# Another order of wide and narrow matmuls inside the units of the seven long sections of a two-layer encoder trunk

## The reference, cut to what matters

```
x = x + attention_layer(rms_norm(x, ...), ...)        # layer 0: its last step is  concat([o_a, o_b]) @ w_out      -> "out0"
x = x + rglru_layer(rms_norm(x, ...), ...)            # layer 1: proj = h @ w_in -> "rec"; (gelu(gate)*y) @ w_out  -> "out1"
x = x + memory_cross_attention(...)                   # both layers
def conv_ffn(h, w_up, conv_w, conv_b, w_down):        # both layers
    u = causal_depthwise_conv(h @ w_up, conv_w, conv_b)          # "up0", "up1"
    val, gate = jnp.split(u, 2, axis=-1)
    return (jax.nn.gelu(gate) * val) @ w_down                    # "down0", "down1"
```

## Time and profile before

| what | value |
|---|---|
| median of 3 runs | 2329.73 us (2328.11 to 2332.1) |
| the profiled execution's own time | 2328.69 us |
| its span | 2327.0 us |
| TensorE (PE) matmul busy | 2299.9 us, 99% |
| VectorE (DVE) busy | 1582.4 us, 68% |
| ScalarE (ACT) busy | 1237.3 us, 53% |
| mean share of the 16 DMA engines | about 55% |
| granted TensorE clock | 0.999 of full, so 2.4 GHz |

### The profile page before, as it was taken

How to read it: one execution, slowest core, us unless ns; L and a number is a source line. 1 busy time by engine, 2 the same in 40 slices (tenths; PEclk the granted TensorE clock), 3 DMA queues, 4 the chain that set the end, 5 groups by cost and what they waited for, 6 DMA issues and landing times.

```text
span 2327.0 us, 38309 instructions
## 1 busy us (share of the span) xinstructions
PE 2299.9 (99%) x13164; PEld 2003.6 (86%) x13164; DVE 1582.4 (68%) x1958; ACT 1237.3 (53%) x1692; POOL 222.8 (10%) x201
## 2 busy tenths in 40 slices
PE   7999999999999999999999999999999999999999
PEld 6888888998888888888888888898888888888888
DVE  7766776677777777755555778667777777774444
ACT  5655555565555555544444776555555555553332
POOL 7630001230000000000000100212000000000000
PEclk9999999999999999999999999999999999999999
DMA  7555435544555555565555555645555555556554
GB/s 279 183 197 195 137 119 175 178 148 163 186 187 199 185 180 191 188 204 189 189 189 181 181 190 181 199 135 174 181 191 188 199 180 180 197 186 202 187 188 159
DMA packets 118077, 426.93 MB, mean 183 GB/s; under 512 B 13504, under 2 KB 14144, under 8 KB 117872
## 3 DMA queue, kind: packets, MB, share of 16 engines
q1 hardware_dynamic: 116640, 418.36, 53.9%
q0 software_dynamic: 1360, 7.52, 1.0%
HBM read 423.73 MB, written 2.10 MB: 183 GB/s over the span
## 4 chain that ended last, share of the span: by engine, by line
PE 93%; POOL 2%; DVE 2%; ACT 1%; issue 1%; DMA 1%; SPq 0%; ACTq 0%; POOLq 0%; DVEq 0%
PE ps L339 51%; PE ps L343 25%; PE ps L373 9%; PE ps L324 2%; PE ps L360 2%; POOL sq L427 1%; POOL acc L428 1%; PE ps L616 1%; PE ps L803 1%; ACT w_hi L306 1%; DVE w_lo L312 0%; PE ps L601 0%; DMA memT<-in_mem_t 0%; PE ps L686 0%; POOL rq L1741 0%
## 5 line engine op out<-in xcount | busy, mean ns | idle before, releaser
L312 DVE TENSOR_TENSOR w_lo<-raw,w_hi 128x1024 fp32r<-128x1024 f32 x788 | 963.6, 1243 | 498.6 <-ACT w_hi L306 494.4
L306 ACT ACTIVATE w_hi<-raw 128x1024 fp32r<-128x1024 f32 x788 | 812.1, 1054 | 572.9 <-PE ps L343 424.7
L339 PE MATMUL ps<-xg_hl,w_hi 128*128 128x512 f32 x3328 | 1048.1, 396 | 6.6 <-DVE w_lo L312 6.6
L343 PEld LDWEIGHTS ps<-xg_hl,w_lo 128*128 128x128 f32 x3328 | 625.9, 188 | 148.1
L343 PE MATMUL ps<-xg_hl,w_lo 128*128 128x256 f32 x3328 | 654.3, 278 | 0.0
L339 PE MATMUL ps<-a_hl,w_hi 128*128 128x512 f32 x1920 | 603.1, 395 | 0.6 <-DVE a_hl L1395 0.6
L339 PEld LDWEIGHTS ps<-xg_hl,w_hi 128*128 128x128 f32 x3328 | 507.6, 189 | 7.6 <-DVE w_lo L312 7.4
L343 PEld LDWEIGHTS ps<-a_hl,w_lo 128*128 128x128 f32 x1920 | 360.7, 188 | 85.2
L343 PE MATMUL ps<-a_hl,w_lo 128*128 128x256 f32 x1920 | 377.2, 278 | 0.0
L339 PEld LDWEIGHTS ps<-a_hl,w_hi 128*128 128x128 f32 x1920 | 292.3, 189 | 0.7 <-DVE w_lo L312 0.7
L1109 ACT ACTIVATE y_buf<-u_buf,fconv 128x256 f32<-128x256 f32 x176 | 96.4, 595 | 230.3 <-DVE u_buf L1570 230.3
(11 more groups left out here) (193 smaller groups left out, 1556.3 us busy)
## 6 DMA issues: line engine op xcount, KB each, us to landing
raw<-in_w_stream SPq DMA_DIRECT2D x788, 512.0 KB, 4.1
bias<-in_rel_bias POOLq DMA_DIRECT2D x4, 768.0 KB, 6.1
memT<-in_mem_t POOLq DMA_DIRECT2D x1, 2048.0 KB, 9.1
gate_w<-in_gate_w POOLq DMA_DIRECT2D x4, 512.0 KB, 3.9
out_t<-xT SPq DMA_DIRECT2D x8, 256.0 KB, 4.5
xT<-in_x_t SPq DMA_DIRECT2D x2, 512.0 KB, 8.7
xT<-in_x_t SPq DMA_DIRECT2D x2, 384.0 KB, 6.0
xT<-in_x_t SPq DMA_DIRECT2D x1, 256.0 KB, 3.4
```

The lines of the kernel that those rows point to most:

```text
L306: nc.scalar.activation(w_hi[:, s, :], raw[:, s, :], ACT.Copy).then_inc(hi_done, 1)
L312: nc.vector.tensor_tensor(w_lo[:, s, :], raw[:, s, :], w_hi[:, s, :].bitcast(F), ALU.subtract).then_inc(lo_done, 1)
L339: nc.tensor.matmul(ps[:, bank + m, :], w_hi[:, s, w], both, start=start and k == ks[0], stop=False, skip_group_check=True)
L343: last = nc.tensor.matmul(ps[:, bank + m, SEQ:2 * SEQ], w_lo[:, s, w], x[:, xk, 0, :], start=False, stop=stop and k == ks[-1], skip_group_ ...
```

## The change

`pair_part` and its wrapper become one function, `pair_unit`, which takes a string of 16 letters and issues the wide and narrow matmuls in that order. The n-th `h` is always the n-th block of high weights and the n-th `l` the n-th block of low weights; so the same 16 matmuls are issued with the same operands. Each section gets a string of its own; `out1` and the woven units keep the old one.

```
+PLAIN = "hhll" * 4
+ORDERS = {"out0": "hlhhll" * 2 + "hlhl", "up0": "hhll" + "hl" * 6, "down0": "hhhlll" * 2 + "hhll", "rec": "hh" + "lh" * 6 + "ll",
+          "out1": PLAIN, "up1": "hhlhll" * 2 + "hhll", "down1": "hlhlhhll" * 2}
...
-        def pair_part(pe, c, k0, ks, x, bank, start, stop, i=None, per=0, ready=None, done=True):
-
-            s = c % SLOTS
+        def pair_unit(pe, c, k0, x, bank, start, stop, i=None, per=0, ready=None, order=PLAIN):
+
+            s, at_h, at_l = c % SLOTS, 0, 0
             pe.wait_ge(lo_done, times(c + 1, i, per))
...
+            for kind in order:
+                if kind == "h":
+                    k, m = at_h // 2, at_h % 2
+                    if ready and m == 0:
+                        ready(k0 + k)
+                    nc.tensor.matmul(ps[:, bank + m, :], w_hi[:, s, at_h * P:(at_h + 1) * P],
+                                     x[:, k0 + k, :, :].rearrange("p a n -> p (a n)"), start=start and k == 0,
                                      stop=False, skip_group_check=True)
...
+                    at_h += 1
+                else:
+                    k, m = at_l // 2, at_l % 2
+                    last = nc.tensor.matmul(ps[:, bank + m, SEQ:2 * SEQ], w_lo[:, s, at_l * P:(at_l + 1) * P], x[:, k0 + k, 0, :],
+                                            start=False, stop=stop and k == 3, skip_group_check=True)
+                    at_l += 1
+            last.then_inc(pe_unit, 1)
```

More of the change, by code:

```diff
@@ L326, in feature_unit @@
             last.then_inc(pe_unit, 1)
-        def pair_part(pe, c, k0, ks, x, bank, start, stop, i=None, per=0, ready=None, done=True):
-            s = c % SLOTS
+        def pair_unit(pe, c, k0, x, bank, start, stop, i=None, per=0, ready=None, order=PLAIN):
+            s, at_h, at_l = c % SLOTS, 0, 0
             pe.wait_ge(lo_done, times(c + 1, i, per))
[L332 to L339, removed]
-                                     stop=False, skip_group_check=True)
[L341 to L349, removed]
+            for kind in order:
[5 more added lines that the diff above has]
+                                     x[:, k0 + k, :, :].rearrange("p a n -> p (a n)"), start=start and k == 0,
+                                     stop=False, skip_group_check=True)
+                    at_h += 1
[5 more added lines that the diff above has]
+            last.then_inc(pe_unit, 1)
         def sum_part(pe, c, ks, x, bank, ready, done=True):
@@ L663, in blocks @@
                             pair_unit(pe, c0 + q * units + u, 4 * u, a_hl, 2 * (q % 2), u == 0, u == units - 1,
-                                      i, 4 * units, tile_there)
+                                      i, 4 * units, tile_there, ORDERS[name])
                 if name == "out1":
@@ L670, in out_section @@
                             pe.wait_ge(proj_free, fblock[name] + q + 1)
-                        pair_unit(pe, c0 + x, 4 * u, a_hl, 2 * q, u == 0, u == units - 1, ready=tile_there)
+                        pair_unit(pe, c0 + x, 4 * u, a_hl, 2 * q, u == 0, u == units - 1, ready=tile_there, order=ORDERS[name])
                     blocks(None, (3,))
@@ L776, in body @@
                                 pe.wait_ge(rbc_ready, BC.index(n) + 1)
-                        pair_unit(pe, c0 + u, k, xg_hl, 2 * (q % 2), k == 0, k == KT - 4, i, 4 * U_BLOCK)
+                        pair_unit(pe, c0 + u, k, xg_hl, 2 * (q % 2), k == 0, k == KT - 4, i, 4 * U_BLOCK, order=ORDERS[f"up{l}"])
                 body(None)
@@ L792, in block_units @@
                         pair_unit(pe, c + u, k, xg_hl, 2 * (q % 2), k == 0, k == KT - 4, i, 4 * U_BLOCK,
-                                  ready if q == 0 else None)
+                                  ready if q == 0 else None, ORDERS["rec"])
                         if hook:
```

## The result

The changed kernel takes 2340.59 us (median of 4 runs) against 2329.93 us (median of 4) for the one before: 10.7 us more, a ratio of 1.0044 with a 95% interval from 1.0031 to 1.0057. It is slower, by less than half a per cent, but clear of the noise and beyond the 4.7 us that the prediction took as the least that can be told. The profiled execution has a span of 2336.8 us, 9.8 more than before.

The account below looks back on a forecast made before the run. TensorE's single sequence of matmuls was taken to bound the kernel. 1016 more turns at 3.3 ns, 3.4 us, added to 2329.7 gave a median of 2333.1 us; the 8-in-10 range was 2319 to 2343 us.

Parts of the forecast that it names:

- The bound: Whole kernel: one sequence of matmuls on TensorE, busy 2299.9 of 2327.0 us, so any change of matmul distance is paid in full.
- The costs taken at nothing: Activation waits, slots given back to ScalarE, DMA, other queues and consecutive matmuls in one PSUM bank: each costed at nothing.
- ScalarE's 1.5 us: ScalarE's waits for TensorE's slots, read as 1.5 us a unit on average, against a unit-length change of less than 1%.
- two other helpers: token_unit and feature_unit: consecutive matmuls to one PSUM bank run there at the undisturbed 0.2267 and 0.1200 us.
- The way: Whole kernel: slower, by 3.4 us, to a median of 2333.1 us.
- the forecast's own: Range of the turns forecast alone, 2331 to 2336.5 us; that forecast had chance 0.40.
- 1016 more turns at 3.3 ns: Six reordered sections: more turns from narrow back to wide, each priced at 3.3 ns, 3.4 us more in all.
- the place to look: Down0, the only section with fewer turns: forecast 2.783 us a unit; being slowest would show the turns step wrong.
- Rival 1: Lone narrow matmuls, most in up0 and rec, cover the next weights too briefly: 10.4 us slower, 2340.1 us; chance 0.21.
- Rival 2: The surcharge belongs to a pair's second wide matmul, alternating avoids it: 9 us less, 2320.7 us; chance 0.23.
- Rival 3: Each kind of matmul has its price in this function whatever its neighbours: no change, 2329.7 us; chance 0.16.
- The rule of the Trainium skill: A back-to-back matmul takes its columns at 2.4 GHz and about 2.5 ns; by it order would be worth nothing.

Follow-up runs that it names:

- rec and down1: Changed kernel with only these two sections keeping their new strings, the other five back at hhll: 2334.98 us, ratio 1.0026 to the kernel before.
- eight and eight: Changed kernel with all seven sections running eight wide and then eight narrow matmuls in a unit: 2334.54 us, ratio 1.0021 to the kernel before.
- the settled kernel: Changed kernel with hl eight times everywhere, but each loop body opens with eight wide, eight narrow, then a unit of hhll and six hl: 2321.81 us, ratio 0.9969.
- its counterpart: Same as the settled kernel, but the second unit of each loop body has hhll twice and hl four times: 2354.27 us, ratio 1.0106.
- the experiment on the banks: Changed kernel's strings, but from a unit's second k tile on the two narrow matmuls of a k tile change places: 2339.19 us, one execution.
- strict alternation: Changed kernel with all seven sections running hl eight times in a unit: eight executions from 2322.75 to 2351.29 us, ratio 1.0043 to the kernel before.

## Why the prediction was right or wrong, point by point

**The bound: right.** TensorE's distances are paid in full: 9.1 us of unit prices became 9.8 us of span and 10.7 us of median, and in the timed experiments the sum of the unit prices and the measured difference agree to about 1 us (4.5 and 4.8 us for rec and down1; 4.3 and 5.5 for eight and eight; 8.3 and 8.4 less for the settled kernel, 23.7 and 24.1 more for its counterpart).

**The costs taken at nothing: right.** Waits, splits and the mean clock are as before. One reading was off without harm: ScalarE's 1.5 us is 424.7 / 279, so per wait and not per unit; over 640 units it is 0.66 us, still far above the 0.033 us by which the dearest unit grew. That neighbours in one bank are free was argued from two other helpers; the experiment on the banks shows it.

**The way: right; the size: wrong.** 3.4 us were forecast and 10.7 came, inside the whole range (2319 to 2343 us) but outside the forecast's own (2331 to 2336.5); "slower" by more than 4.7 us had a chance of 0.32 there, "within" 0.47. The term that was mis-sized is "1016 more turns at 3.3 ns": in place of its 3.4 us the units grew by 9.1 us. It failed at its first step, the division of the 13.3 ns that `hhll` costs above its parts by its four turns, as if each turn had a price of its own. A turn has none. It costs nothing in the short rhythm (`hl` x 8: 2.7733 us with eight turns, the sum of the parts alone), 6.7 ns in the long one (353.3 ns a pair against 346.7), 3.3 in `hhll`, and 20 in eight and eight (2.7933 less 2.7733, one turn). Down0 was named as the place to look: fewest turns, forecast 2.783, measured 2.797, not the dearest section but dearer than before. Up0 met its forecast, 2.797, by accident, as the mean of two rhythms that are 40 ns apart.

**The rows could not settle it.** `hhll` goes through two states in the kernel before, 233 236 116 113 (698 ns) and 232 231 113 119 (695), one after the other. A price per group of 0.6967 us is the mean of the two, and which of the two comes last decides what the next stretch costs. The wide pairs, 469 and 463 ns, stand in the earlier trace rows as 0.47 and 0.46 us in turn. But two decimals can't tell this from rounding: an even 0.4667 us would give such a mix as well. It takes the starts to 1 ns.

**Rival 1, slower by lone narrows: its time came out (2340.1 forecast, 2340.6 measured), its mechanism did not.** Up0 should have been 2.815 and is 2.797; down0 has no lone narrow and pays 10 ns; up1 has two a unit and pays the same 10; and strict alternation has eight and can cost less than `hhll`. That the total fitted is chance.

**Rival 2, faster by alternation: half right in its price, wrong in its mechanism.** The alternating stretches do come down to 346.7 ns a pair, its lesser end (3.5 us less). But a wide matmul that stands alone keeps its surcharge: it takes 233 or 231 ns in the short rhythm and up to 241 in the long one, not 226.7. The pair costs no more than its parts alone only because the narrow ones keep their rebate as well, 117 and 112 ns in place of 120. That the settled kernel's 2321.81 us lies beside the 2320.7 of this rival is chance, since the rival's figure was for 608 units with some lone ones and a middle between two bounds. To be faster takes the short rhythm in nearly all units; the change's strings give it in half of up0's units and lose it again.

**Rival 3, order does not matter: wrong.** The two kernels that settle the rhythm, with the same matmuls in almost the same order, are 32.5 us apart, 51 ns for each of 640 units. The rule of the Trainium skill that the prediction set beside it (TensorE: Matmul & The Clock Gate, Wait, 56 ns, not 53.3 ns?), about 2.5 ns beyond the columns for each back-to-back matmul, doesn't hold here in size, nor does what the prediction drew from it, that order would be free: the measured cost above the stream is 13.3 ns in uniform sequences and the short rhythm and 16.7 in the long one (1060 less 3 x 320 ns of streams, over six).

**What stays open.** What the state is. It is carried from unit to unit across waits that are met and loop branches, and it doesn't show in the last distance: behind 236 113 (long rhythm) as behind 231 112 (short) comes an `hhll`, once as 233 236 116 113 and once as 232 231 113 119. Nor is it shown what part the eight narrow matmuls play: no kernel here settles with an `hhll` alone, and in the changed kernel's up0, where every unit begins with `hhll`, both of its forms come in turn. The unit prices of whole cycles (2.7733, 2.7867, 2.7933, 2.8000, 2.8067, 2.8133 us) are multiples of 3.33 ns; why is open. Nor can the runs tell matmuls from weight loads as the cause, since each matmul has one load, which starts 2 to 5 ns after the matmul ahead of it wherever there is no wait.

## What to carry to other kernels

Where TensorE is the bound and its matmuls differ in width, price a sequence as a whole, from the distances of a stretch that already runs in it; a price per neighbour or per turn does not add up, since the same sequence can settle in two rhythms 2% apart. Look for periods in the distances, from starts to 1 ns, before averaging over them. If a sequence has a fast and a slow rhythm, put a fixed lead-in in every loop body (here eight wide, eight narrow, one `hhll`), or its time may scatter from one execution to the next.

## What the runs showed that I had not expected

- One kernel, one chip, 28.5 us between its executions (2322.75 to 2351.29 us) at a granted clock of 0.998 to 1.000. In the profiled one the rhythm is picked up anew behind waits and other matmuls, sometimes short and sometimes long. That the others differ for the same reason is an inference: an estimate from the unit prices gives 2320.5 us with all 640 units short (2329.0 less 640 x 13.3 ns) and 2354.6 with all long (2329.0 and 640 x 40 ns), and all eight lie between.
- A lead-in of 20 matmuls (eight wide, eight narrow, one `hhll`) sets the rhythm: 38 of 38 short, and with the next four matmuls in another order 38 of 38 long.
- A long run of one width is not the cheapest way (2.7933 us a unit), though its later matmuls are at their undisturbed price: behind eight narrow ones it takes five wide ones before the distance is 227 ns again.
- With the settled alternation the kernel is 0.3% faster than before (0.9957 to 0.9980): 2321.81 us.
